# Gate products of a gated linear recurrence: three fp32r matmuls of split operands in place of one fp32 matmul

## The chip, the cores and the metric

The kernel runs on one core of one Trainium2 chip. The metric is device time in microseconds (us), the median of three runs. TensorE (PE) multiplies, VectorE (DVE), ScalarE (ACT) and GpSimd (POOL) do elementwise work, and SyncE (SP) issues most of the loads. PEld is TensorE's loading of stationary operands.

## The reference

One layer of a residual block on 256 tokens of width 2048, in fp32: RMSNorm, one wide input projection, three branches (forgetting attention, a recurrence, attention into 256 memory rows), a gated merge, an output projection, and a feed-forward block of hidden width 5632. The change is in the recurrence branch, of width 1024 in 8 blocks of 128:

```
xr = causal_depthwise_conv(lx, w_lru_conv, b_lru_conv)            # 4 taps
r      = sigmoid(einsum('bsni,nij->bsnj', xb, w_a) + b_a)         # xb: xr in 8 blocks of 128
i_gate = sigmoid(einsum('bsni,nij->bsnj', xb, w_x) + b_x)
log_a = 8 * r * log_sigmoid(lam);  a = exp(log_a)
u = sqrt(-expm1(2 * log_a)) * (i_gate * xr)
h_t = a_t * h_(t-1) + u_t                                         # scan over the 256 tokens
y_lru = h * gelu(lg)
```

## The kernel before

**Weights come in units.** A unit is 512 KB of fp32 weights. SP loads it into one of four slots of `raw`; ACT copies it to the high part (`split` on ACT, fp32r, L666), DVE subtracts to get the low part (`split` on DVE, L1021), and TensorE multiplies three of the four combinations of high and low parts. ACT may copy unit u only when TensorE is done with unit u-4 (`act.wait_ge(pe_units, u - 3)`), so the two elementwise engines work up to about four units ahead of TensorE. A unit of the phases of 256 columns, the recurrence's own projections ("lru") among them, is 16 matmuls, for each of four contraction steps two with 512 moving columns and two with 256; a unit of the phases of 512 columns ("mk", "mq", "v", ...) is 12 matmuls of 512 columns. All of them are recorded at L362, in the helper `mm`, and write `psG`.

**The recurrence runs in four instances m = 0 to 3, of 256 channels each.** Instance m has two groups of four units (x-branch, gate branch); what follows on the elementwise engines and the gate products is interleaved by hand with the next eight units. Every engine executes its list in order. In the lists, "offset o" means: behind the split of unit `start + o`, where `start` is the first unit behind those of instance m. TensorE runs the gate products behind the second of these units (`lru_hooks`, `{1: gates_}`), waits for the taps and for the gate weights, and writes them to `psM` with four fp32 matmuls of 256 columns (each is two records in the trace).

The order on ACT and DVE around them, for instance m with m-1 still running:

- offset 0, ACT: `conv0_`, the first tap of the convolution, into `lru_xr` (L769).
- offset 1, DVE: for m-1 `recurrence` and `gated_y` (offset 9 of m-1), then `taps` of m, six operations (L1108); the last one raises `lru_taps`.
- offset 2: ACT split, then for m-1 `lru_hi` (L801). DVE split, then for m-1 `lru_lo` (L1143).
- offset 3: ACT `copy_low` (L674), split, `gelu_square` (L776). DVE `add_low` (L1032), split, nothing more.
- offset 5 and later: ACT `gate_tanh` reads the gate products, and log_a, exps, root, scan and so on follow.

For the first instance, the second memory-attention instance is what is still running: DVE's `attention_lo` (L1097) stands behind the split of offset 3.

POOL's list for an instance is: load the gate weights into `lru_rg` (two DMAs, L1512, behind the gate products of m-1), then two operations of the GeLU polynomial behind `gelu_square` (L1518 and L1520), then `a_sq` (L1522).

Of the kernel before, what the change touches and what calls it, by code (L numbers as in the profile page):

```python
# [6 lines left out]
ALU = mybir.AluOpType  # L7
ACT = mybir.ActivationFunctionType
F32 = mybir.dt.float32
F32R = mybir.dt.float32r  # L10
AX_X = mybir.AxisListType.X

P = 128
T = 256
# [102 lines left out]
def side_count(kind, m, engine, step):  # L117

    return m * LEN[kind][engine] + (BASE[kind][engine] + (STEP[kind][engine][step] if step else 0))


def at(const, i, coef):

    return const if i is None else i * coef + const


def hybrid_layer_kernel(nc, xT, x_rows, memT, first_data, par, shapes_const, w_units, w_ff, w_rg, out):
    with ExitStack() as ctx:
# [4 lines left out]
        def sb(name, shape, offset, dt=F32):  # L133
            return nc.alloc_sbuf_tensor_at(name, shape, dt, offset=SB0 + int(offset))

        def sem(name):
            return ctx.enter_context(nc.semaphore(name))
# [6 lines left out]
        def wide_before(g):  # L144

            return sum(name in WIDE for name, _, _, _ in GROUPS[:g])
# [6 lines left out]
        M0, G_0, T0 = 144 * KB + 256, 176 * KB + 256, 192 * KB + 256  # L153
# [38 lines left out]
        lru = {}  # L192
        for n in ["lg", "rg", "xr", "ra", "a", "aa", "tn", "ix", "hs", "gg"]:
            shape = [P, 2, 2, P] if n == "rg" else [P, 2, T]
            lru[n] = sb(f"lru_{n}", shape, _o)
            _o += 2 * KB

        dec = {n: sb(f"dec_{n}", [8, T], G_0 + (12 + j) * KB) for j, n in enumerate(["z", "e", "u", "r"])}
        dec_l = sb("dec_l", [8, T], T0 + 2 * KB + 512)
# [48 lines left out]
        psM = ctx.enter_context(nc.psum_tensor("psM", [P, 4, 512], F32))  # L248
# [10 lines left out]
        gain_in, par_in, const_in, ff_in, rg_in = sem("gain_in"), sem("par_in"), sem("const_in"), sem("ff_in"), sem("rg_in")  # L259
# [11 lines left out]
        lam_act, lam_dve = sem("lam_act"), sem("lam_dve")  # L271
        c_out, c_in = sem("c_out"), sem("c_in")
        lru_conv0, lru_taps = sem("lru_conv0"), sem("lru_taps")
        gate_ready = sem("gate_ready")
        gated, acc_added, merged_hi, merged_lo = sem("gated"), sem("acc_added"), sem("merged_hi"), sem("merged_lo")
        x_tok_in = sem("x_tok_in")
# [14 lines left out]
        def columns(w):  # L291

            return slice(w * 512, (w + 1) * 512)
# [5 lines left out]
        def is_zero(m):  # L299

            return isinstance(m, int) and m == 0

        def f32(ap):
            return ap.bitcast(F32)
# [55 lines left out]
        def _(pe):  # L360
            def mm(*a, **kw):
                return nc.tensor.matmul(*a, skip_group_check=True, **kw)  # L362
# [62 lines left out]
            def side_waits(**need):  # L425
                for e, v in need.items():
                    if not is_zero(v):
                        pe.wait_ge(side[e], v)

            def done(ins):  # L430
                ins.then_inc(side["pe"], 1)
# [72 lines left out]

            def lru_hooks(m):
                def gates_():
                    pe.wait_ge(rg_in, at(32, m, 32))
                    pe.wait_ge(lru_taps, at(3, m, 3))

                    side_waits(act=side_count("lru", m - 1, "act", "gate_tanh"))  # L510
                    for j in range(2):
                        for b in range(2):
                            ins = mm(psM[:, j, b * T:(b + 1) * T], lru["rg"][:, j, b], lru["xr"][:, b], start=True, stop=True)
                    done(ins)
                return {1: gates_}

# [113 lines left out]
            for t in range(2):  # L630
                for k in range(2):
                    x_hl = hidden_op(FT - 2 + k)
                    for x_part, w_part in ((0, 0), (0, 1), (1, 0)):
                        ins = mm(psG[:, 2 + t, :], x_hl[:, x_part, t * P:t * P + P], W[:, s, 2 * k:2 * k + 2, w_part],
                                 start=False, stop=k == 1 and x_part == 1)
# [23 lines left out]
        def _(act):  # L659
# [16 lines left out]
            def wait(**need):  # L676
                for e, v in need.items():
                    if not is_zero(v):
                        act.wait_ge(side[e], v)

            def done(ins):
                ins.then_inc(side["act"], 1)
# [79 lines left out]
            L = lru  # L762

            def conv0_(kind, m):
# [5 lines left out]
                                               bias=p1("b_lconv", m * 2 + b), scale=p1("w_lconv", m * 2 + (3 * BT + b)))  # L770
                ins.then_inc(lru_conv0, 1)

            def gelu_square(kind, m):
                wait(**{e: side_count("lru", m, e, None) for e in ("pe", "dve", "act", "pool")})
                act.wait_ge(evac_done, at(G0["lru"] + 2, m, 2))
                done(nc.scalar.activation(L["gg"][:], L["lg"][:], ACT.Square))  # L776
# [30 lines left out]
            def decay_ln(kind, m):  # L807
# [2 lines left out]

            softmax = {7: [exp], 10: [weights_copied], 11: [attention_hi]}
            steps_at = {"normed": {3: [norm_squares]}, "turned": {0: [turned_copied]}, "mem": softmax, "fox": softmax,
                        "lru": {0: [conv0_], 3: [gelu_square], 5: [gate_tanh], 7: [exps, gelu_tanh], 9: [lru_root], 10: [lru_hi]},
                        "decay": {6: [decay_exp], 8: [decay_ln]}}
            hooks = build_hooks(steps_at)

# [197 lines left out]
        def _(dve):  # L1014
            V = nc.vector
# [18 lines left out]
            def wait(**need):  # L1034
                for e, v in need.items():
                    if not is_zero(v):
                        dve.wait_ge(side[e], v)

            def done(ins):
                ins.then_inc(side["dve"], 1)  # L1040
# [58 lines left out]
            L = lru  # L1099

            def taps(kind, m):
                for n in (2, 1, 0):
# [6 lines left out]
                                                     L["xr"][:, b], ALU.mult, ALU.add)  # L1109
                    ins.then_inc(lru_taps, 1)  # L1110

            def log_a(kind, m):
                wait(act=side_count("lru", m, "act", "gate_tanh"))
                for b in range(2):
                    ins = V.tensor_scalar(L["ra"][:, b], L["ra"][:, b], 1.0, ls4[:, bass.ds(m * 2 + b, 1)], ALU.add, ALU.mult)
                done(ins)

                done(V.scalar_tensor_tensor(L["ix"][:], L["ix"][:], 1.0, L["xr"][:], ALU.add, ALU.mult))
# [72 lines left out]
            def decay_bias1(kind, m):  # L1191
# [2 lines left out]

            steps_at = {"normed": {3: [norm]}, "mem": {7: [row_max, weights], 11: [attention_lo]},
                        "fox": {7: [row_max, weights], 11: [attention_lo]},
                        "lru": {1: [taps], 6: [log_a], 8: [decay_sq], 9: [recurrence, gated_y], 10: [lru_lo]},
                        "decay": {5: [decay_z], 7: [decay_one_plus], 8: [decay_inverse], 9: [decay_c], 14: [decay_bias0], 15: [decay_bias1]}}
            hooks = build_hooks(steps_at)

# [220 lines left out]
            for w in range(2):  # L1421
                ins = V.memset(up_pad[w][:, :, 0:2], 0.0)
# [54 lines left out]
            for w in range(4):  # L1477
                per = FT // 2
                for u in range(U0["down"] + per * w + 4, U0["down"] + per * (w + 1) + 4):
                    if u == U0["down"] + per * (w + 1) + 3 and w < 3:  # L1480
                        dve.wait_ge(pe_units, u - 3)
                        b = 2 * (w % 2)
# [10 lines left out]
        @block.gpsimd  # L1493
        def _(pool):
            G = nc.gpsimd

            def wait(**need):
                for e, v in need.items():
                    if not is_zero(v):
                        pool.wait_ge(side[e], v)  # L1500

            def done(ins):
                ins.then_inc(side["pool"], 1)


            def load_gates(m):

                if is_zero(m):
                    pool.wait_ge(pe_units, U0["mq"])
                wait(pe=side_count("lru", m, "pe", None))  # L1510
                for j in range(2):
                    G.dma_start(lru["rg"][:, j], w_rg[j, bass.ds(m * 2, 2)].rearrange("b n c -> n b c")).then_inc(rg_in, 16)  # L1512

            L = lru
            def lru_instance(m):
                load_gates(m)
                wait(act=side_count("lru", m, "act", "gelu_square"))
                done(G.tensor_scalar(L["gg"][:], L["gg"][:], GELU_C, 1.0, ALU.mult, ALU.add))  # L1518
                wait(pool=side_count("lru", m, "pool", "gelu_poly"))
                done(G.tensor_tensor(L["gg"][:], L["gg"][:], L["lg"][:], ALU.mult))  # L1520
                wait(act=side_count("lru", m, "act", "exps"))
                done(G.tensor_tensor(L["aa"][:], L["a"][:], L["a"][:], ALU.mult))  # L1522


            for m in range(4):
                lru_instance(m)

            wait(dve=side_count("decay", 0, "dve", "c"))
            G.dma_start(c_rows, dec["u"][:]).then_inc(c_out, 16)
            pool.wait_ge(c_out, 16)  # L1530
            G.dma_start(c_all[:], c_rows.rearrange("(a h) t -> a h t", a=1).to_broadcast([P, 8, T])).then_inc(c_in, 16)

            pool.wait_ge(x_scaled, 4)
            G.dma_start(x_tok[:], x_rows).then_inc(x_tok_in, 16)

            for w in range(3):
                pool.wait_ge(evac_done, G0["down"] + w + 1)
                G.dma_start(out_rows[:, :, columns(w)], x_tok[:, :, columns(w)]).then_inc(out_stored, 16)
            pool.wait_ge(out_stored, 48)
# [96 lines left out]
```

## Time and profile before

| what | value |
|---|---|
| median of 3 runs | 1627.57 us (1627.21 to 1627.66) |
| the profiled execution | 1627.56 us, span of its instructions 1625.8 us |
| PE busy | 1619.8 us (100%), 8564 matmul records |
| DVE, ACT, POOL busy | 1050.5 us, 869.0 us, 25.3 us |
| chain that ended last | PE 99% |

The span runs from the first instruction to the last. An engine's busy time counts its records; a matmul's record is longer than the distance to the next one, since matmuls overlap. The chain that ended last is followed back from the last instruction to what released it at each step, so its pieces on PE give start-to-start times. Of the chain, 96% is weight products into `psG` at L362, 2% products into `psM` at L362, the gate products among them.

### The profile page before, as it was taken

Reading aid. Unit: us, or ns where it says so; the run is one execution under the profiler, and the core shown is the slowest. Engines: PE = TensorE matmul, PEld = TensorE weight load, DVE = VectorE, ACT = ScalarE, POOL = GpSimd, SP = SyncE. Lnnn points to the kernel's source line nnn. Section 1 sums busy time; section 2 is a strip of 40 time slices with the busy share of each in tenths; the row PEclk is TensorE's granted clock in tenths of the full one; section 3 lists DMA queues with packets and bytes.
Section 4 is the critical chain, followed back from the end, with each engine's and each line's share of the span. In section 5 each row is a group of like instructions: output and inputs, shape, how many; then the busy total and the mean of one; then the engine's idle time right before and its main releaser. Section 6 shows DMA issues by size and latency. Waiting matters only on the chain.

```text
span 1625.8 us, 24820 instructions
## 1 busy us (share of the span) xinstructions
PE 1619.8 (100%) x8564; PEld 1391.6 (86%) x8564; DVE 1050.5 (65%) x1257; ACT 869.0 (53%) x1192; POOL 25.3 (2%) x30
## 2 busy tenths in 40 slices
PE   9999999999999999999999999999999999999999
PEld 8888888888888888888888888888888888888887
DVE  6865678655656575565755777777777777544443
ACT  7665676456554544554544655555555555433332
POOL 0000121000000000000000000000000000000000
PEclk9999999999999999999999999999999999999999
DMA  9554455755556555555565555555655655665663
GB/s 349 183 196 152 158 168 188 259 175 157 160 188 194 190 184 194 182 192 193 181 195 184 176 184 193 197 187 184 203 176 188 206 186 186 201 205 194 206 207 115
DMA packets 85280, 309.58 MB, mean 190 GB/s; under 512 B 9832, under 2 KB 10352, under 8 KB 84976
## 3 DMA queue, kind: packets, MB, share of 16 engines
q1 hardware_dynamic: 83952, 303.14, 56.3%
q0 software_dynamic: 1136, 5.78, 1.0%
q8 instruction: 32, 0.52, 0.1%
q14 instruction: 16, 0.13, 0.0%
q10 hardware_dynamic: 144, 0.01, 0.0%
HBM read 306.78 MB, written 2.11 MB: 190 GB/s over the span
## 4 chain that ended last, share of the span: by engine, by line
PE 99%; DMA 0%; ACT 0%; DVE 0%; issue 0%; ACTq 0%
PE psG L362 96%; PE psM L362 2%; PE psM L447 0%; DMA par_sb<-par 0%; PE psM L601 0%; PE psM L483 0%; ACT fox_square L695 0%; PE psM L481 0%; DVE normed L1059 0%; ACT W L666 0%; DVE x_tok L1490 0%; ACT XM L833 0%; ACT head_rms L707 0%; DVE head_rms L1054 0%; ACT L707 0%
## 5 line engine op out<-in xcount | busy, mean ns | idle before, releaser
L1021 DVE TENSOR_TENSOR W<-raw,W 128x1024 fp32r<-128x1024 f32 x566 | 686.5, 1225 | 380.9 <-ACT W L666 378.3
L362 PE MATMUL psG<-X,W 128*128 128x512 f32 (+1 forms) x4864 | 848.5, 336 | 0.0
L362 PEld LDWEIGHTS psG<-X,W 128*128 128x128 f32 x4864 | 741.2, 188 | 104.1
L666 ACT ACTIVATE W<-raw 128x1024 fp32r<-128x1024 f32 x566 | 589.7, 1054 | 392.3 <-PE psG L362 378.8
L362 PE MATMUL psG<-W,hidden 128*128 128x512 f32 x1056 | 239.5, 389 | 0.0
L362 PEld LDWEIGHTS psG<-W,hidden 128*128 128x128 f32 x1056 | 198.2, 188 | 41.0
L362 PE MATMUL psG<-W,X 128*128 128x512 f32 x768 | 178.6, 392 | 0.0
L362 PEld LDWEIGHTS psG<-W,X 128*128 128x128 f32 x768 | 143.5, 188 | 29.5
L674 ACT ACTIVATE low<-psG 128x512 f32<-128x512 f32 x100 | 59.7, 597 | 149.1 <-PE psG L362 149.1
L362 PE MATMUL psG<-Y,W 128*128 x768 | 133.3, 335 | 0.0
L362 PEld LDWEIGHTS psG<-Y,W 128*128 128x128 f32 x768 | 116.9, 188 | 16.0
L1437 DVE SCALAR_TENSOR_TENSOR up_c<-up_pad,par_sb,up_c 128x256 f32<-128x256 f32 x176 | 77.5, 481 | 42.3 <-ACT up_c L974 36.3
L362 PE MATMUL psG<-W,XM 128*128 128x512 f32 x384 | 88.8, 392 | 0.2 <-ACT XM L833 0.2
L362 PE MATMUL psG<-W,merged 128*128 128x512 f32 x384 | 88.1, 390 | 0.0
L362 PEld LDWEIGHTS psG<-W,XM 128*128 128x128 f32 x384 | 72.2, 189 | 15.6 <-ACT XM L833 0.5
L362 PEld LDWEIGHTS psG<-W,merged 128*128 128x128 f32 x384 | 71.8, 188 | 14.7
L974 ACT ACTIVATE up_c<-up_pad,par_sb 128x256 f32<-128x256 f32 x88 | 48.2, 595 | 60.8 <-DVE up_pad L1429 60.8
L1000 ACT ACTIVATE hidden<-up_c 128x512 f32 (+1 forms) x22 | 13.9, 632 | 65.3 <-DVE up_c L1466 65.3
L1032 DVE TENSOR_TENSOR up_pad<-psG,low 128x512 f32<-128x512 f32 x44 | 30.4, 691 | 25.2 <-ACT low L674 25.2
L1032 DVE TENSOR_TENSOR gates<-psG,low 128x512 f32<-128x512 f32 x24 | 16.6, 691 | 27.8 <-ACT low L674 27.8
L1032 DVE TENSOR_TENSOR yd<-psG,low 128x512 f32<-128x512 f32 x24 | 16.6, 691 | 22.6 <-ACT low L674 22.6
L1429 DVE TENSOR_TENSOR up_pad<-up_pad,rstd 128x512 f32<-128x512 f32 x44 | 30.3, 688 | 0.8
(191 smaller groups left out, 553.1 us busy)
## 6 DMA issues: line engine op xcount, KB each, us to landing
raw<-w_units SPq DMA_DIRECT2D x566, 512.0 KB, 4.0
xs<-xT SPq DMA_DIRECT2D x4, 512.0 KB, 8.0
x_tok<-x_rows POOLq DMA_DIRECT2D x1, 2048.0 KB, 12.2
mem_raw<-first_data SPq DMA_DIRECT2D x3, 512.0 KB, 4.8
mem_raw<-memT SPq DMA_DIRECT2D x3, 512.0 KB, 7.9
out<-x_tok POOLq DMA_DIRECT2D x3, 512.0 KB, 4.2
lru_rg<-w_rg POOLq DMA_DIRECT2D x8, 128.0 KB, 3.9
c_all<-c_rows POOLq DMA_DIRECT2D x1, 1024.0 KB, 6.6
```

Of the source, the lines that this page charges most:

```text
L362: return nc.tensor.matmul(*a, skip_group_check=True, **kw)
L666: nc.scalar.activation(W[:, s, :, 0], raw[:, s], ACT.Copy).then_inc(hi_done, 1)
L674: nc.scalar.activation(low[:, g % 2], psG[:, b:b + 2, T:], ACT.Copy).then_inc(low_copied, 1)
L974: ins = nc.scalar.activation(up_c[w][:, t], up_pad[w][:, t, 2:], ACT.Identity, bias=p1("b_fconv", i * 2 + (w * FT + t)), scale=p1("w_fconv ...
L1000: nc.scalar.activation(hidden[:, bass.ds(i * 2, 2), 0, :], up_c[1][:], ACT.Copy).then_inc(hidden_hi, 1)
L1021: V.tensor_tensor(W[:, s, :, 1], raw[:, s], f32(W[:, s, :, 0]), ALU.subtract).then_inc(lo_done, 1)
L1032: V.tensor_tensor(dst, psG[:, b:b + 2, 0:T], low[:, g % 2], ALU.add).then_inc(evac_done, 1)
L1429: V.tensor_tensor(up_pad[w][:, :, 2:], up_pad[w][:, :, 2:], rstd2.rearrange("p (a t) -> p a t", a=1).to_broadcast([P, 2, T]), ALU.mult).th ...
L1437: ins = V.scalar_tensor_tensor(up_c[w][:, t], up_pad[w][:, t, n:n + T], p1("w_fconv", i * 2 + (n * 2 * FT + w * FT + t)), up_c[w][:, t], A ...
```

## The change

The gate weights and the convolved input of the recurrence are split into high and low parts, in two new buffers `lru_w` and `lru_x` (fp32r), and each fp32 gate product becomes three fp32r matmuls of 256 columns (high·high, high·low, low·high), accumulated in the same half of a bank. ACT makes the high parts at offset 2 (two copies of 256 elements per partition for the weights, one of 512 for the input), DVE the low parts at offset 3 (two subtractions of 256, one of 512). TensorE waits for the low parts in place of the loaded weights and the taps. POOL's load of the next gate weights waits for the low weights of the instance before in place of its gate products, and the first load no longer waits for TensorE's steps of the memory attention.

```diff
+        lru_w = sb("lru_w", [P, 2, 2, 2, P], M0 + 89 * 256, F32R)
+        lru_x = sb("lru_x", [P, 2, 2, T], M0 + 105 * 256 + 64, F32R)
...
             def lru_hooks(m):
                 def gates_():
-                    pe.wait_ge(rg_in, at(32, m, 32))
-                    pe.wait_ge(lru_taps, at(3, m, 3))
+                    pe.wait_ge(lru_w_lo, at(1, m, 1))
+                    pe.wait_ge(lru_x_lo, at(1, m, 1))
...
                     for j in range(2):
                         for b in range(2):
-                            ins = mm(psM[:, j, b * T:(b + 1) * T], lru["rg"][:, j, b], lru["xr"][:, b], start=True, stop=True)
+                            for w_part, x_part in ((0, 0), (0, 1), (1, 0)):
+                                ins = mm(psM[:, j, b * T:(b + 1) * T], lru_w[:, j, b, w_part], lru_x[:, b, x_part],
+                                         start=w_part + x_part == 0, stop=w_part == 1)
                     done(ins)
...
+            def gate_weights_hi(kind, m):
+                act.wait_ge(rg_in, at(32, m, 32))
+                for j in range(2):
+                    ins = nc.scalar.activation(lru_w[:, j, :, 0], L["rg"][:, j], ACT.Copy)
+                ins.then_inc(lru_w_hi, 1)
+
+            def gate_input_hi(kind, m):
+                act.wait_ge(lru_taps, at(3, m, 3))
+                nc.scalar.activation(lru_x[:, :, 0], L["xr"][:], ACT.Copy).then_inc(lru_x_hi, 1)
...
-                        "lru": {0: [conv0_], 3: [gelu_square], 5: [gate_tanh], 7: [exps, gelu_tanh], 9: [lru_root], 10: [lru_hi]},
+                        "lru": {0: [conv0_], 2: [gate_weights_hi, gate_input_hi], 3: [gelu_square], 5: [gate_tanh], 7: [exps, gelu_tanh], 9: [lru_root], 10: [lru_hi]},
...
+            def gate_weights_lo(kind, m):
+                dve.wait_ge(lru_w_hi, at(1, m, 1))
+                for j in range(2):
+                    ins = V.tensor_tensor(lru_w[:, j, :, 1], L["rg"][:, j], f32(lru_w[:, j, :, 0]), ALU.subtract)
+                ins.then_inc(lru_w_lo, 1)
+
+            def gate_input_lo(kind, m):
+                dve.wait_ge(lru_x_hi, at(1, m, 1))
+                V.tensor_tensor(lru_x[:, :, 1], L["xr"][:], f32(lru_x[:, :, 0]), ALU.subtract).then_inc(lru_x_lo, 1)
...
-                        "lru": {1: [taps], 6: [log_a], 8: [decay_sq], 9: [recurrence, gated_y], 10: [lru_lo]},
+                        "lru": {1: [taps], 3: [gate_weights_lo, gate_input_lo], 6: [log_a], 8: [decay_sq], 9: [recurrence, gated_y], 10: [lru_lo]},
...
                 if is_zero(m):
                     pool.wait_ge(pe_units, U0["mq"])
-                wait(pe=side_count("lru", m, "pe", None))
+                else:
+                    pool.wait_ge(lru_w_lo, m)
                 for j in range(2):
                     G.dma_start(lru["rg"][:, j], w_rg[j, bass.ds(m * 2, 2)].rearrange("b n c -> n b c")).then_inc(rg_in, 16)
```

## Rows read from the trace of the kernel before

**Rows 1.** Page, part 1: busy time of TensorE, share of the span, instructions.

```profile
PE 1619.8 (100%) x8564; PEld 1391.6 (86%) x8564; DVE 1050.5 (65%) x1257; ACT 869.0 (53%) x1192; POOL 25.3 (2%) x30
```

**Rows 2.** Chain that ended last, in time order: start us, us, what.

```profile
84.38 21.78 PE psG L362 x96
...
184.98 1.73 PE psM L362 x8
186.71 22.30 PE psG L362 x128
209.01 1.73 PE psM L362 x8
...
234.77 22.19 PE psG L362 x120
```

**Rows 3.** Waits of TensorE over the span: us in total, times, longest.

```profile
PE psM L447 <- DVE normed L1059: 1.0, 1, 1.0
```

**Rows 4.** Instructions on the tile of the gate weights: ns min/median/max, first and last start.

```profile
L362 PE MATMUL psM<-lru_xr,lru_rg x32: 377/379/382, 184.8 to 258.3; 128*128 128x256 f32 x32
L1512 POOL DMA_DIRECT2D lru_rg<-w_rg x8: 720/752/847, 180.1 to 245.7; - x8
...
DMA to landing us min/median/max: 2.8/3.9/5.5
```

**Rows 5.** Timeline of DVE: start us, us, instruction, count, idle before.

```profile
180.51 1.23 DVE L1097 TENSOR_TENSOR Y<-psM,Y 128x1024 fp32r<-128x1024 f32 x1 [1.72 <-ACT Y L760]
...
204.25 2.92 DVE L1108 SCALAR_TENSOR_TENSOR lru_xr<-lx_pad,par_sb,lru_xr 128x256 f32<-128x256 f32 x6
207.09 1.22 DVE L1021 TENSOR_TENSOR W<-raw,W 128x1024 fp32r<-128x1024 f32 x1
208.23 0.69 DVE L1143 TENSOR_TENSOR Y<-lru_hs,Y 128x512 f32 x1
208.83 0.68 DVE L1032 TENSOR_TENSOR lru_lg<-psG,low 128x512 f32<-128x512 f32 x1
209.43 1.22 DVE L1021 TENSOR_TENSOR W<-raw,W 128x1024 fp32r<-128x1024 f32 x1
```

**Rows 6.** Timeline of ACT around the second instance's gate products.

```profile
204.47 0.64 ACT L801 ACTIVATE Y<-lru_hs 128x512 f32 x1 [2.53 <-DVE lru_hs L1138]
205.01 0.58 ACT L674 ACTIVATE low<-psG 128x512 f32<-128x512 f32 x1
205.49 1.05 ACT L666 ACTIVATE W<-raw 128x1024 fp32r<-128x1024 f32 x1
```

**Rows 7.** Timeline of POOL in the recurrence.

```profile
182.55 0.61 POOL L1518 TENSOR_SCALAR lru_gg<-lru_gg 128x512 f32<-128x512 f32 x1 [0.90 <-ACT lru_gg L776]
...
210.28 0.84 POOL L1518 TENSOR_SCALAR lru_gg<-lru_gg 128x512 f32<-128x512 f32 x1 [12.72 <-ACT lru_gg L776]
211.21 1.29 POOL L1520 TENSOR_TENSOR lru_gg<-lru_gg,lru_lg 128x512 f32<-128x512 f32 x1
...
259.28 2.33 POOL L1520 TENSOR_TENSOR lru_gg<-lru_gg,lru_lg 128x512 f32<-128x512 f32 x1
```

**Rows 8.** Timeline of DVE beside the last of these POOL operations.

```profile
259.23 3.46 DVE L1021 TENSOR_TENSOR W<-raw,W 128x1024 fp32r<-128x1024 f32 x2 [0.51 <-ACT W L666]
```

**Rows 9.** Chain that ended last, around TensorE's one later wait.

```profile
327.36 1.23 DVE normed L1059
...
328.73 1.06 PE psM L447 x8
...
351.59 0.87 PE psM L447 x8
```

**Rows 10.** Timeline of TensorE, its first instructions.

```profile
1.07 4.21 PE L362 MATMUL psM<-ones 128*128 128x128 f32 x18 [1.07 <-DVE ones L1208]
```

**Rows 11.** Stretches after TensorE's last matmul: busy of PE, PEld, DVE, ACT, POOL, clock, DMA.

```profile
1622.20:1624.60 2.40, 0.00 (x0) 0.00 (x0) 0.68 (x1) 0.00 (x0) 0.00 (x0) 1.00 0.58 219
1624.70:1625.70 1.00, 0.00 (x0) 0.00 (x0) 0.00 (x0) 0.00 (x0) 0.00 (x0) 0.50 0.00 0
```

More of the change, by code:

```diff
@@ L273, in hybrid_layer_kernel @@
         lru_conv0, lru_taps = sem("lru_conv0"), sem("lru_taps")
+        lru_w_hi, lru_w_lo, lru_x_hi, lru_x_lo = sem("lru_w_hi"), sem("lru_w_lo"), sem("lru_x_hi"), sem("lru_x_lo")
         gate_ready = sem("gate_ready")
```

## The prediction

> **What bounds the kernel now.** I read the page's busy times first: TensorE fills the span [rows 1]. The list of its waits then shows, behind the first microseconds, a single one, of 1.0 us near 328 us [rows 3]. So time comes off or on in two ways alone: the start-to-start time of TensorE's own work, or a new wait of TensorE. Everything on ACT, DVE, POOL and the queues is free as long as TensorE doesn't wait for it. The chain in time order gives the start-to-start times: the eight fp32 records of one instance's gate products take 1.73 us, at 184.98 and at 209.01, with 22.30 us of weight products between [rows 2]. No wait stands at any of the four instances, so what feeds the gate products is early now. How early is the question, and the timelines of DVE and ACT answer it: the last tap of the second instance ends at 204.25 + 2.92 = 207.17 [rows 5], and TensorE comes to the gate products at 209.01 [rows 2]. The slack is 1.84 us.
>
> **TensorE's own part.** The profile gives 379 ns to one fp32 record [rows 4], but the records overlap, and the chain has 1.73 / 8 = 0.216 us for one. The new matmuls have fp32r operands and 256 moving columns. Such ones stand in the units of the recurrence's projection, mixed half and half with 512-column ones: 22.30 us for 128 is 0.174 us each, and the 512-column ones alone take 21.78 / 96 = 0.227 us [rows 2]. So one of 256 columns takes 2 x 0.174 - 0.227 = 0.121 us, and twelve take 1.46 us: 0.27 us less per instance, 1.1 us for four. The mixed units change the bank between matmuls and the new ones stay in one half bank for three; no row has that at 256 columns. From above I bound it by the fp32 record's 0.216 us (twelve: 2.59 us, 4.5 us more than my value for four instances), from below by nothing less than half a 512-column one, 0.113 us (0.4 us less for four). I take 0.121, since operands and columns are those of the row.
>
> **The added operations on ACT.** At offset 2 ACT now makes two copies of 256 elements behind `lru_hi`, which starts at 204.47, the next instruction at 205.01 [rows 6]. A copy of 512 took 0.64 us there, so two of 256 take at most 1.3 us, and end before the last tap at 207.17: that wait hides them. The gate weights are there: their two DMAs start right behind `a_sq`, the last pair by 245.7 for an instance whose gate products start near 257, and land in at most 5.5 us [rows 4]. The copy of the input then waits for the last tap and starts near 207.25; the next instruction starts 0.54 us after such a copy and 0.48 us after a `copy_low` (205.01 less 204.47, 205.49 less 205.01) [rows 6]. So `copy_low` moves from 205.01 to about 207.8 and ends near 208.4, and the split of offset 3 moves from 205.49 to about 208.3 and ends near 209.35. In the queue behind the waiting copy are just these two, and DVE waits for both: its `add_low` starts at 208.83 and its split at 209.43 [rows 5]. Both are met, the second by less than 0.1 us. ACT's part costs nothing, and a tenth more of lateness would cost a tenth.
>
> **The added operations on DVE: here the change costs.** The low parts stand behind the split of offset 3. From the taps on DVE works without a gap: split 207.09, `lru_lo` 208.23, `add_low` 208.83, split 209.43 [rows 5]. That last split already starts later than TensorE's arrival at the gate products, and the three new subtractions come after it. The step from one operation to the next is 1.14 us for 1024 elements and 0.60 for 512 [rows 5], so 0.33 for 256. The first low part can start at 209.43 + 1.14 = 210.57, and alone the three would end at 210.57 + 2 x 0.33 + 0.69 = 211.92.
>
> They aren't alone. At 210.28 POOL starts the two GeLU operations of the same instance, which run until 212.5, in a stretch in which DVE is idle now [rows 7]. Where the two engines meet, they take turns: the second POOL operation takes 1.29 us beside an idle DVE, but 2.33 us at 259.28 [rows 7], when DVE's two splits beside it take 3.46 us in place of about 2.36 [rows 8]. The first one takes 0.61 alone and 0.84 when it comes during a split (210.28, split until 210.65) [rows 5, 7]. The sums show a turn by whole instructions: the second split ends at 262.69, which is 1.08 us behind the POOL operation that came before it and ended at 261.61, a whole split less 0.14. With that: POOL's first operation ends at 211.12 and the first subtraction at 211.12 + 0.42 - 0.14 = 211.40. POOL's second arrives at 211.21 during it and, as at 259.28, ends 1.15 us behind the DVE operation that it waited for, at 212.55. The second subtraction ends at 212.83, and the third, started 0.09 us before that, at 213.43. Without turns it would be 211.92; I take 213.43. The Trainium skill's "SBUF — State Buffer", section "SBUF: two separate sides", says the same as a rule: the pair of ports that DVE and GpSimd share is an exclusive lock for a whole instruction. The trace agrees with it at 259.28; by the rule the low input ends where I put it, and without it the total below would be some 4.5 us less.
>
> TensorE then starts 0.14 us after DVE's record (327.36 + 1.23 to 328.73) and loses 0.19 us of overlap on the first matmuls (1.06 in place of 0.87) [rows 9]. The gate products end at 213.43 + 0.14 + 0.19 + 1.46 = 215.22, against 209.01 + 1.73 = 210.74: 4.48 us later. TensorE stands still for about 4.6 us.
>
> **Which instances, and does it add up?** The chain from the end of one instance's gate products to the next one's taps is the same for each (from 186.71 to 207.17), and ACT's splits in it wait for TensorE, so the whole pattern moves with the stall; nothing is caught up, since TensorE has no other wait in this phase to absorb it. The second and third instances cost 4.48 each, the fourth 4.59, because its way without a stall is 22.19 us and not 22.30 [rows 2]. The first is free: there DVE's `attention_lo` starts at 180.51, the split of offset 3 is long done, and the low parts end by 180.51 + 1.14 + 1.35 = 183.0, or 183.6 with a turn of POOL's 0.61 us between [rows 5, 7], before 184.98 [rows 2]; it saves its 0.27. Sum: 2 x 4.48 + 4.59 - 0.27 = 13.3 us. POOL's earlier load for the first instance, and its changed wait, have nothing behind them that TensorE waits for.
>
> **The clock.** No matmul is recorded from 1622.2 on; the granted clock still reads 1.00 until 1624.6 and 0.50 from 1624.7 [rows 11], so a rest of 2.5 us was enough to bring it from 2.4 to 1.2 GHz there. The rest here would be 4.6 us, and I expect the clock to fall in most of the three. What a return costs is seen at the start only: 18 fp32 records of 128 columns take 4.21 us [rows 10]. A full-clock record of as many columns is 0.87 / 8 = 0.109 us [rows 9], so the 18 should take 1.96, and 2.25 us were lost. For each of the three stalls I bound it by 0 and 2.25 us and take 1.5, nearer to the upper end since the rest exceeds 2.5 us: 4.5 us together. The Trainium skill's "TensorE: Matmul & The Clock Gate", section "Why this matters for your kernels", warns that idle gaps between bursts of matmuls throw the clock back to its half; the trace agrees at its end, where the clock reads 0.50.
>
> **Forecast.** The profiled execution took 1627.56 us, its span 1625.8 and 1.8 around it; the median of the runs is 1627.57, so no correction is needed. 1627.56 + 13.3 + 4.5 = 1645.4 us.
>
> **The rivals.**
> (1) Turns as above, but the clock holds: 1640.9 us. For it: a single rest of 4.6 us between dense matmuls is in no row.
> (2) DVE and POOL don't take turns on these small subtractions, or POOL's operations come later than now: low input at 211.92, 3 us of rest, 2 x 2.97 + 3.08 - 0.27 = 8.75, so 1636.3 us, and up to 1643 with the clock's loss. Against it: rows 7 and 8.
> (3) The stall doesn't come: the low parts are made within the 1.84 us behind the last tap, and the kernel is 1.1 us faster, 1626.5 us, within what a measurement can tell. For that DVE would have to make them before the 3.5 us of `split`, `lru_lo`, `add_low` and `split` that the list puts first; the point that decides is whether the third subtraction ends before 209.0. Against it stand the list and [rows 5].
> (4) The new matmuls take 0.216 us each in one half bank: 4.5 us more, about 1650 us with the forecast's other terms.
>
> **How the numbers follow.** The forecast's case (turns, clock falls at least once; 1642 to 1648.5) gets 0.45, rival 1 0.18, rival 2 0.20, rival 3 0.05, rival 4 0.05, and 0.07 is left for what I don't see. The range from 1636.0 to 1649.0 takes in the forecast's case and rivals 1 and 2 and leaves out rivals 3 and 4 and the rest. A measurement of this kernel can tell about 0.2%, 3.3 us, from no change. Only rival 3 is within that: same 0.05, faster 0.01, slower 0.94.
>
> **What would show each step.** In the changed kernel's profile: a wait of TensorE at `psM` for the low input, three times 4 to 5 us, none at the first instance; DVE's two subtractions of 256 with a gap or a long record between them beside POOL's L1520; the gate products as 12 records in about 1.5 us at full clock; a granted clock below 1.00 in the stretch behind each stall. A stall near 3 us would say that the turns are wrong, none at all that the order on DVE was misread, and four stalls that the first instance isn't free.

## The result, and the profile after

The changed kernel takes 1640.43 us, the kernel before 1627.66 us beside it (medians of seven runs each): ratio 1.0078, 95% interval 1.0066 to 1.009. That is 12.8 us more, inside the range of 1636.0 to 1649.0 and 5 us below the forecast of 1645.4. The first profile of the changed kernel fell in a disturbed execution (mean granted clock 0.85), so the rows below are from a second run of the same file, the first experiment (1639.1 us, profiled execution 1639.14, span 1637.4). Line numbers have moved: L362 is L365, L666 is L671, L1021 is L1036; the new subtractions are L1130 (weights) and L1135 (input).

The list of TensorE's waits in the changed kernel, which answers to [rows 3]:

```profile
PE psM L365 <- DVE lru_x L1135: 6.3, 2, 3.2
PE psM L365 <- DVE lru_w L1130: 3.1, 1, 3.1
...
PE psM L450 <- DVE normed L1074: 1.0, 1, 1.0
```

Three waits of 3.1 to 3.2 us are new, all at the gate products. The chain that ended last shows where they stand (start, us, what); [rows 2] are the same places before:

```profile
184.88 1.42 PE psM L365 x12
186.30 11.17 PE psG L365 x64
...
211.78 1.68 PE psM L365 x12
213.45 11.17 PE psG L365 x64
...
238.93 1.63 PE psM L365 x12
240.55 11.16 PE psG L365 x64
...
265.86 2.90 PE psM L365 x12
268.76 23.26 PE psG L365 x96
```

The first instance has no wait, and its products take 1.42 us in place of 1.73. From the end of one instance's products to the end of the next one's it was 24.03 us (186.71 to 210.74) and is 27.15 (186.30 to 213.45), then 27.10, then 28.21 where it was 23.92. The 96 matmuls behind the last take 23.26 us in place of 21.78. The sum is -0.31 + 3.12 + 3.07 + 4.29 + 1.48 = 11.65 us, all of the 11.6 us by which the span grew. The last two terms hold the clock, as the stretches say (PE, PEld, DVE, ACT, POOL, then the granted clock, DMA):

```profile
211.78:213.45 1.67, 1.67 (x13) 1.67 (x14) 1.26 (x1) 1.32 (x2) 1.52 (x2) 1.00 0.74 275
...
265.86:268.76 2.90, 2.90 (x13) 2.90 (x14) 2.17 (x2) 1.34 (x2) 2.82 (x2) 0.50 0.66 237
268.76:271.60 2.84, 2.84 (x9) 2.16 (x8) 0.00 (x0) 1.57 (x4) 1.11 (x1) 0.50 0.83 276
```

Behind the first two waits the clock stays at 2.4 GHz (1.00); behind the third it is at 1.2 GHz (0.50), and twelve products take 2.90 us there.

Why the low input is late is read in the timeline of DVE around the second instance, which answers to [rows 5]:

```profile
203.85 2.93 DVE L1123 SCALAR_TENSOR_TENSOR lru_xr<-lx_pad,par_sb,lru_xr 128x256 f32<-128x256 f32 x6
206.70 1.22 DVE L1036 TENSOR_TENSOR W<-raw,W 128x1024 fp32r<-128x1024 f32 x1
207.84 0.68 DVE L1168 TENSOR_TENSOR Y<-lru_hs,Y 128x512 f32 x1
208.44 0.68 DVE L1047 TENSOR_TENSOR lru_lg<-psG,low 128x512 f32<-128x512 f32 x1
209.04 1.22 DVE L1036 TENSOR_TENSOR W<-raw,W 128x1024 fp32r<-128x1024 f32 x1
210.17 0.75 DVE L1130 TENSOR_TENSOR lru_w<-lru_rg,lru_w 128x256 fp32r<-128x256 f32 x2
210.84 0.68 DVE L1135 TENSOR_TENSOR lru_x<-lru_xr,lru_x 128x512 fp32r<-128x512 f32 x1
```

Four operations stand between the taps and the low parts, without a gap, and the low input ends at 211.52, 7.67 us after the first tap starts. TensorE's matmuls start at 211.78, 0.26 us later. The three subtractions run without a gap too; it is POOL that waits for them (timeline of POOL; [rows 7] before):

```profile
209.89 2.12 POOL L1544 TENSOR_SCALAR lru_gg<-lru_gg 128x512 f32<-128x512 f32 x1 [12.73 <-ACT lru_gg L791]
212.09 1.30 POOL L1546 TENSOR_TENSOR lru_gg<-lru_gg,lru_lg 128x512 f32<-128x512 f32 x1
...
264.12 4.39 POOL L1544 TENSOR_SCALAR lru_gg<-lru_gg 128x512 f32<-128x512 f32 x1 [12.73 <-ACT lru_gg L791]
```

ACT's part, which answers to [rows 6]: the high input starts right behind the last tap, and the two operations behind it come when DVE needs them.

```profile
206.81 0.64 ACT L786 ACTIVATE lru_x<-lru_xr 128x512 fp32r<-128x512 f32 x1 [1.49 <-DVE lru_xr L1123]
207.35 0.58 ACT L679 ACTIVATE low<-psG 128x512 f32<-128x512 f32 x1
207.83 1.05 ACT L671 ACTIVATE W<-raw 128x1024 fp32r<-128x1024 f32 x1
```

### The profile page after: what moved, and what is told of

It is laid out like the page before. It is cut to its first block, busy times and chain, and to the rows that moved or that the text cites. A ratio compares the mean times of both kernels' runs of the same rounds, so it can differ in the third digit from the quotient of the medians.

```text
span 1787.5 us, 24878 instructions
## 1 busy us (share of the span) xinstructions
PE 1775.3 (99%) x8580; PEld 1452.0 (81%) x8580; DVE 1060.1 (59%) x1269; ACT 880.5 (49%) x1204; POOL 28.8 (2%) x30
## 4 chain that ended last, share of the span: by engine, by line
PE 97%; DVE 1%; issue 1%; ACT 1%; DMA 0%; DVEq 0%; ACTq 0%
PE psG L365 93%; PE psM L365 2%; PE psM L450 0%; DVE W L1036 0%; DVE lru_xr L1123 0%; DMA par_sb<-par 0%; PE psM L606 0%; ACT L812 0%; PE psM L486 0%; ACT lru_aa L812 0%; DVE lru_w L1130 0%; DVE lru_hs L1155 0%; DVE lru_ix L1152 0%; ACT fox_square L700 0%; PE psM L484 0%
## 5 line engine op out<-in xcount | busy, mean ns | idle before, releaser
L1036 DVE TENSOR_TENSOR W<-raw,W 128x1024 fp32r<-128x1024 f32 x566 | 690.2, 1227 | 480.6 <-ACT W L671 478.4
L365 PE MATMUL psG<-X,W 128*128 128x512 f32 (+1 forms) x4864 | 922.9, 355 | 0.0
L365 PEld LDWEIGHTS psG<-X,W 128*128 128x128 f32 x4864 | 780.5, 193 | 139.5
L671 ACT ACTIVATE W<-raw 128x1024 fp32r<-128x1024 f32 x566 | 594.4, 1055 | 503.5 <-PE psG L365 494.1
L365 PE MATMUL psG<-W,hidden 128*128 128x512 f32 x1056 | 265.1, 417 | 0.0
L365 PEld LDWEIGHTS psG<-W,hidden 128*128 128x128 f32 x1056 | 202.4, 192 | 62.3
L365 PE MATMUL psG<-W,X 128*128 128x512 f32 x768 | 196.9, 419 | 0.0
L365 PEld LDWEIGHTS psG<-W,X 128*128 128x128 f32 x768 | 146.9, 192 | 44.0
L365 PE MATMUL psG<-Y,W 128*128 x768 | 145.1, 354 | 0.0
L365 PEld LDWEIGHTS psG<-Y,W 128*128 128x128 f32 x768 | 122.9, 192 | 21.9
L365 PE MATMUL psG<-W,XM 128*128 128x512 f32 x384 | 98.1, 420 | 0.4 <-ACT XM L848 0.4
L365 PE MATMUL psG<-W,merged 128*128 128x512 f32 x384 | 97.3, 417 | 0.0
L365 PEld LDWEIGHTS psG<-W,XM 128*128 128x128 f32 x384 | 74.0, 194 | 23.0 <-ACT XM L848 0.7
L365 PEld LDWEIGHTS psG<-W,merged 128*128 128x128 f32 x384 | 73.4, 192 | 22.2
```

The lines of the kernel that those rows point to most:

```text
L671: nc.scalar.activation(W[:, s, :, 0], raw[:, s], ACT.Copy).then_inc(hi_done, 1)
L1036: V.tensor_tensor(W[:, s, :, 1], raw[:, s], f32(W[:, s, :, 0]), ALU.subtract).then_inc(lo_done, 1)
```

## The experiments

In all of them the medians and ratios are against runs of the kernel before on the same chip (1627.40 to 1627.56 us).

**The changed kernel again, for its profile.**

> The changed kernel once more, for a profile at full clock. Order theory: the three low-part subtractions stand behind four other DVE operations, run without a gap, and end 7.7 us after the first tap starts (211.9 in the times of the kernel before); three waits of TensorE of about 3 us cost 8.75 us with the 0.27 us won at the first instance, and the clock falls to 0.50 behind some of them, which costs the other 4 us of about 12.8: some 1640.4 us. Rival, turns theory: DVE and POOL take turns, the low input ends near 213.4, the three waits are 4.5 us each (13.3 us in all), and the granted clock stays at 1.00: 1640.9 us. Second rival, load theory: no long waits, but all units of the recurrence are longer because ACT and DVE have 12 operations more.

Measured: 1639.1 us, ratio 1.0071 (1.0056 to 1.0087). Three waits of 3.13 to 3.18 us, low input 7.67 us behind the first tap, DVE without a gap: the order theory, and against the turns. The clock fell behind one wait in the profiled execution.

**The added work alone.**

```diff
 def gates_():
-    pe.wait_ge(lru_w_lo, at(1, m, 1))
-    pe.wait_ge(lru_x_lo, at(1, m, 1))
+    pe.wait_ge(rg_in, at(32, m, 32))
+    pe.wait_ge(lru_taps, at(3, m, 3))
...
-            for w_part, x_part in ((0, 0), (0, 1), (1, 0)):
-                ins = mm(psM[:, j, b * T:(b + 1) * T], lru_w[:, j, b, w_part], lru_x[:, b, x_part],
-                         start=w_part + x_part == 0, stop=w_part == 1)
+            ins = mm(psM[:, j, b * T:(b + 1) * T], lru["rg"][:, j, b], lru["xr"][:, b], start=True, stop=True)
```

(In this kernel and the next, POOL's load of the gate weights also waits for the gate products of the instance before, as it did.)

> All twelve added ACT and DVE operations stay where the change puts them, but TensorE multiplies in fp32 as before and waits for the taps and the loaded weights as before. Order theory and turns theory: the work alone costs nothing, 1627.7 us, no wait at the gate products. Load theory: most of the 12.8 us stays, above 1635 us.

Measured: 1627.51 us, ratio 0.9999 (0.9989 to 1.0008), no wait at the gate products. Six more operations per instance on ACT and DVE (24 in all, twelve on each engine) cost nothing where TensorE doesn't wait for them. The load theory falls.

**The wait alone.** The products are fp32 as before, the waits are the changed kernel's.

```diff
             pe.wait_ge(lru_w_lo, at(1, m, 1))
             pe.wait_ge(lru_x_lo, at(1, m, 1))
...
-            for w_part, x_part in ((0, 0), (0, 1), (1, 0)):
...
+            ins = mm(psM[:, j, b * T:(b + 1) * T], lru["rg"][:, j, b], lru["xr"][:, b], start=True, stop=True)
```

> TensorE waits for the low parts as in the change, but multiplies in fp32 as before. Order theory and turns theory: the wait alone is the cost; each instance's products take 0.27 us more than in the change, 1.1 us in all: about 1641.5 us. If the new products were part of the cost, it would be below the changed kernel's 1640.4 us.

Measured: 1643.39 us, ratio 1.0094 (1.0079 to 1.0109). The wait brings all of the cost, and the products win some of it back; the waits are the same 3.1 to 3.2 us. It is 2 us more than was expected. One source shows in the profiled execution, the longest of the four (1645.54 us): the products of all three instances behind a wait take 1.7 to 2.2 times the 1.73 us of the first, with a mean granted clock of 0.50 to 0.64 over them. How often the clock fell in the other three isn't shown. That execution also lost time ahead of the first instance, which has nothing to do with the waits: its products start at 186.71, in the kernel before at 184.98 [rows 2].

```profile
186.71 1.73 PE psM L365 x8
...
213.91 3.01 PE psM L365 x8
...
243.00 3.78 PE psM L365 x8
...
273.11 3.48 PE psM L365 x8
```

**Two operations fewer in front.** One change to the order, on DVE:

```diff
-"lru": {1: [taps], 3: [gate_weights_lo, gate_input_lo], ...
+"lru": {1: [taps], 2: [gate_weights_lo, gate_input_lo], ...
```

> The low parts on DVE move from behind the split of offset 3 to behind the split of offset 2: two operations, an add of 0.60 and a split of 1.14 us, no longer stand before them. Order theory: the low input ends 1.74 us earlier, three waits of about 1.4 us in place of 3.1; 2 x 1.23 + 1.34 - 0.27 = 3.5 us of stall, and with a rest that short the clock holds: 1630.9 us. If the clock falls all the same, up to 1634 us. If the order on DVE weren't the cause, it stays at 1639 us.

Measured: 1631.27 us, ratio 1.0024 (1.0014 to 1.0034), waits of 1.40 to 1.45 us, mean granted clock 1.00. Moving two operations of 1.74 us in sum from before the low parts to behind them takes 1.7 us off each wait, and the clock holds after a rest of 1.4 us.

**The clock's share.** The loop over the instances is written out, so that filling products can stand at the second to fourth instance alone. In both kernels the wait for `gate_tanh` of the instance before moves ahead of the filling:

```diff
-with pe.Fori(1, 4) as i:
-    plain("lru", i, lru_hooks(i - 1))
+for i in range(1, 4):
+    plain("lru", i, lru_hooks(i - 1, fill=12 if i > 1 else 0))
...
+for _ in range(fill):
+    mm(psM[:, 3, 0:P], ones[:], ones[:], start=True, stop=True)
 pe.wait_ge(lru_w_lo, at(1, m, 1))
```

> The changed kernel with TensorE's three instances of the recurrence loop written out, and 12 fp32 products of ones by ones (24 records of 0.109 us, 2.6 us) into an unused bank ahead of the wait at the second to fourth instance, so that TensorE works through most of the 3.1 us of rest. Clock theory: the clock stays at 1.00, the stall itself stays, 1627.4 + 8.75 = 1636.2 us, about 3 us below the changed kernel. Rival: the clock costs nothing and the rest of the 11.7 us is stall; then it stays at 1639 us or above.

> The same written-out loop without the filling products, as the other half of the comparison: as the changed kernel, 1639 to 1640 us, with at least one stretch of granted clock 0.50 behind a stall. If writing out the loop alone changes the time, this shows it.

Measured: 1637.24 us with the filling (ratio 1.0059, 1.0046 to 1.0073; five runs from 1636.05 to 1637.66), 1641.15 us without (1.0084, 1.007 to 1.0098; 1638.92 to 1644.26), which is 1 us above what was expected. The timeline of TensorE with the filling shows 24 records and then a rest of 0.38 us only:

```profile
208.54 2.84 PE L365 MATMUL psM<-ones 128*128 128x128 f32 x24
211.77 1.65 PE L365 MATMUL psM<-lru_x,lru_w 128*128 128x256 f32 x12 [0.38 <-DVE lru_x L1136]
```

The low input comes no earlier, TensorE gains no time by the filling, and the kernel is 3.9 us faster, since the clock stays at 1.00 (mean of each of the five runs). Against the changed kernel's own two medians, 1640.43 and 1639.1, it is 3.2 and 1.9 us, so the size is rough; no run with the filling is as long as the shortest without it. Without it the stretches of the profiled execution (1644.26 us) show the wait, in which PE has nothing, and a lower clock behind each of the three:

```profile
210.50:213.40 2.90, 0.00 (x0) 0.00 (x0) 2.81 (x5) 2.60 (x4) 1.72 (x1) 1.00 0.62 195
213.46:216.50 3.04, 3.04 (x17) 2.85 (x18) 2.52 (x2) 2.47 (x5) 1.63 (x2) 0.71 0.42 158
242.03:245.00 2.97, 2.96 (x13) 2.97 (x14) 2.45 (x2) 1.43 (x2) 1.62 (x2) 0.50 0.42 157
270.60:277.00 6.40, 6.40 (x23) 5.63 (x24) 2.12 (x2) 2.85 (x6) 3.88 (x2) 0.56 0.68 234
```

The chain of the same execution gives the price of a fall:

```profile
186.68 1.41 PE psM L365 x12
...
213.46 1.84 PE psM L365 x12
215.31 12.53 PE psG L365 x64
...
242.03 2.88 PE psM L365 x12
244.92 11.47 PE psG L365 x64
```

At full clock the same products and the 64 matmuls behind them take 1.68 + 11.17 and 1.63 + 11.16 us (the changed kernel's chain above), so the first two falls cost 1.5 and 1.6 us. Its products start 1.8 us later at the first instance too (186.68, in the changed kernel 184.88), so not all of its 1644.26 us is wait and clock.

The filled kernel's stalls are what was expected: the products of one instance end 27.02 us behind those of the one before, three times, where it was 24.03, 24.03 and 23.92, which less the 0.31 us won at the first makes 8.8 us. It takes 1 us more than 1636.2 and has 1.1 us of waits for weight units, at 329 and 332 us, which the changed kernel lacks; why they come there is not settled.

**Low parts right behind the taps.**

```diff
-ACT "lru": {0: [conv0_], 2: [gate_weights_hi, gate_input_hi], 3: [gelu_square], ...
+ACT "lru": {0: [conv0_], 1: [gate_weights_hi], 2: [gate_input_hi], 3: [gelu_square], ...
-DVE "lru": {1: [taps], 3: [gate_weights_lo, gate_input_lo], ...
+DVE "lru": {1: [taps, gate_weights_lo, gate_input_lo], ...
```

> The high weights move to offset 1 on ACT, and the three low-part subtractions to right behind the taps on DVE, ahead of the split of offset 2. Order theory: the low input ends near 208.5, before TensorE arrives at 208.7 to 209.0; no wait, no fall of the clock, and the cheaper products show: 1627.7 - 4 x 0.27 = 1626.6 us. Turns theory: the same, since POOL starts later than the low parts end. Load theory: the added operations are all still there, so it stays above 1631 us.

Measured: 1628.14 us, ratio 1.0004 (0.9995 to 1.0013). The 11 us of loss are gone, but 1.5 us more than expected stay: the third and fourth instance wait 0.75 us each. In the timeline of ACT, `gelu_square` waits for DVE's add, which the three subtractions have pushed back, and a load of ACT's function table (`ACT_TABLE_LOAD`, 1.28 us), the splits and `gate_tanh` (L797) queue behind it, so that `gate_tanh` starts 1.25 us later than before (214.65 for 213.40). The recurrence of this instance follows from `gate_tanh`, and on DVE it stands in front of the next instance's taps:

```profile
210.78 0.64 ACT L791 ACTIVATE lru_gg<-lru_lg 128x512 f32<-128x512 f32 x1 [1.66 <-DVE lru_lg L1047]
211.44 1.28 ACT L671 ACT_TABLE_LOAD   x1
212.73 2.01 ACT L671 ACTIVATE W<-raw 128x1024 fp32r<-128x1024 f32 x2
214.65 0.81 ACT L797 ACTIVATE lru_ra<-psM,half_ba 128x256 f32<-128x256 f32 x2
```

**The same, with `gelu_square` one unit later.** Twice, the second time for the interval.

```diff
-ACT "lru": {..., 3: [gelu_square], 5: [gate_tanh], ...
+ACT "lru": {..., 4: [gelu_square], 5: [gate_tanh], ...
```

> The order of the run with the low parts right behind the taps, and gelu_square moved from offset 3 to offset 4 on ACT, so that ACT's next splits don't wait behind it for DVE's later add. In that run the third and fourth instance waited 0.75 us each, because gate_tanh came 1.25 us later on ACT than in the kernel before. If that is the cause: no wait of TensorE at the gate products, 1627.4 - 1.1 = 1626.3 us. If the late load of a weight unit is the cause instead, the two waits of 0.75 us stay: 1628 us.

> The order of the run with the low parts behind the taps and gelu_square at offset 4, once more, for the interval: 1626.4 us, 1.0 us less than the kernel before, of which four cheaper gate products (4 x 0.3 us) are the whole. If it was noise, 1627.4 us.

Measured: 1626.44 us (ratio 0.9994, 0.9985 to 1.0003) and 1626.41 us (0.9992, 0.9983 to 1.0001). `gate_tanh` starts at 212.51 in the first and TensorE has no wait at the gate products in either profile. The load of ACT's function table now stands ahead of `gelu_square`, where ACT has time, and no longer behind its wait for DVE:

```profile
208.78 1.28 ACT L671 ACT_TABLE_LOAD   x1
...
211.05 0.61 ACT L791 ACTIVATE lru_gg<-lru_lg 128x512 f32<-128x512 f32 x1
211.56 1.05 ACT L671 ACTIVATE W<-raw 128x1024 fp32r<-128x1024 f32 x1
212.51 0.82 ACT L797 ACTIVATE lru_ra<-psM,half_ba 128x256 f32<-128x256 f32 x2
```

The chain of the first of the two has the four products alone:

```profile
184.77 1.42 PE psM L365 x12
...
208.49 1.51 PE psM L365 x12
...
232.30 1.51 PE psM L365 x12
...
255.99 1.46 PE psM L365 x12
```

They take 5.90 us in place of 4 x 1.73 = 6.92: 1.02 us less, and the medians are 0.96 and 1.15 us less. This order has the lowest medians of all; each interval by itself still reaches past 1, by 0.0003 and 0.0001, so the gain is about 0.06 to 0.07% and at the edge of what can be told.

**Does the kind of POOL's operation decide who goes first?**

```diff
-done(G.tensor_scalar(L["gg"][:], L["gg"][:], GELU_C, 1.0, ALU.mult, ALU.add))
+done(G.tensor_tensor(L["gg"][:], L["gg"][:], L["lg"][:], ALU.mult))
...
-done(G.tensor_tensor(L["gg"][:], L["gg"][:], L["lg"][:], ALU.mult))
+done(G.tensor_tensor(L["gg"][:], L["gg"][:], L["lg"][:], ALU.add))
```

> The changed kernel with POOL's first GeLU operation turned from one with a scalar into one with two input tensors (square times gate, then plus gate; the constant 0.0447 of the cubic term is left out, so the output differs). In the kernel before, an operation with two inputs got its turn between two DVE splits; in the changed kernel the one with a scalar got none and waited 2.1 us until all three subtractions were through. If the kind of operation decides: the first POOL operation runs between the subtractions, the low input ends about 1.2 us later, the waits grow from 3.1 to about 4.3 us, and the time to 1642.5 us or more. If it doesn't decide: POOL's operation waits again, the waits stay at 3.1 us and the time at 1639 to 1640 us.

Measured: 1640.15 us, ratio 1.0077 (1.0061 to 1.0092), waits of 3.1 to 3.2 us. The operation with two inputs waits as well (timelines of POOL and of DVE):

```profile
209.74 2.80 POOL L1544 TENSOR_TENSOR lru_gg<-lru_gg,lru_lg 128x512 f32<-128x512 f32 x1 [12.76 <-ACT lru_gg L791]
```

```profile
210.03 0.76 DVE L1130 TENSOR_TENSOR lru_w<-lru_rg,lru_w 128x256 fp32r<-128x256 f32 x2
210.70 0.69 DVE L1135 TENSOR_TENSOR lru_x<-lru_xr,lru_x 128x512 fp32r<-128x512 f32 x1
```

The kind doesn't decide. In the same profile POOL's second operation, of the same kind, does get its turn between two splits that follow each other without a gap: it takes 2.14 us in place of 1.29, and the two splits 3.78 in place of 2.36 (the first of them also waits for POOL's first operation to end).

```profile
212.61 2.14 POOL L1546 TENSOR_TENSOR lru_gg<-lru_gg,lru_lg 128x512 f32<-128x512 f32 x1
```

```profile
212.05 3.78 DVE L1036 TENSOR_TENSOR W<-raw,W 128x1024 fp32r<-128x1024 f32 x2 [0.66 <-ACT W L671]
```

## Why the prediction was right, and where it was not

**The main step held.** The time is lost where the prediction put it: DVE's list puts the split, `lru_lo`, the add and another split between the taps and the low parts, and the low input misses TensorE at the second to fourth instance, not at the first. Shown from four sides: the work without the wait costs nothing (1627.51), the wait without the new products costs it all (1643.39), two operations fewer in front take 1.7 us off each wait (1631.27), and the low parts in front of all four, with `gelu_square` out of the way, leave none (1626.4).

**The step that failed is the turns of DVE and POOL.** The prediction took 213.43 for the end of the low input, with POOL's two operations between the subtractions, over 211.92 without. Counted from the first tap these are 9.18 and 7.67 us; measured is 7.67. DVE went through split and all three subtractions, and POOL's first operation took 2.12 us in place of 0.84. That was 1.51 us too much at each of three instances, 4.5 us, about the whole miss. Its evidence was one meeting in the trace of before, POOL getting in between two splits near 259 us [rows 7, 8]. Such turns exist in the later runs too (2.14 us of POOL's second operation in the last experiment, 2.33 us at the fourth instance of the run with two operations fewer in front), but at the three subtractions POOL got none in any profile of the changed kernel's order. What decides between the two outcomes stays open. The prediction named the sign itself, a stall near 3 us: the waits are 3.1 to 3.2 us. What happened was the second rival, with the clock's loss, for which the text gave 1636.3 to 1643. That the measured time lies in the forecast's range is owed to the range, which took this rival in; the forecast's own case, 1642 to 1648.5, missed it. Rival 1's 1640.9 comes nearest to the median by luck: it has turns at the subtractions and a clock that holds, and the runs of the changed kernel show neither.

**The restart** was sized a little low: 0.26 us from DVE's record to the matmuls where 0.14 was taken, and 0.26 us of lost overlap (1.68 less 1.42) where 0.19 was. Each stall cost 3.07 to 3.12 us at full clock against 2.97 in the sum without turns.

**The clock** fell as forecast, though over a shorter rest and not behind each stall; the sum of its loss came near the forecast's although in the profiles some falls were missing and one cost more than its bound. The stalls alone make about -0.31 + 3.12 + 3.07 + 3.2 = 9.1 us (3.2 for the fourth, like the others plus its 0.11); what the median has above that is 12.8 - 9.1 = 3.7 us, where 4.5 was taken, and the filling products give 3.9 us back. It varies between executions: the profile with 1639.14 us has one fall, that with 1644.26 us has three. A single fall cost 1.5 and 1.6 us behind the first two waits of the latter, as taken, but about 2.6 us behind the third wait of the former (4.29 - 3.2 + 1.48), more than the 2.25 us that the prediction set as an upper bound from the kernel's start.

**The products** were right within a tenth of a us: 1.42 to 1.51 us, forecast 1.46. Staying in one half bank for three matmuls has no price that shows. **ACT's part** was right: the copy of the input waits for the tap, and the two operations behind it come just in time.

## What to carry to other kernels

Cheaper matmuls are worth what they save only if their operands are ready as early as before: count, on the engine that makes the operands, every instruction that the order puts between the last input and the new operation, and set it against the slack (here 1.84 us of slack, and 3.5 us of other work put in front of 1.35 us of new work). The new work itself was free; its place in the queue cost 12.8 us, and a better place turned it into a gain of 1.0 us. A stall of TensorE can cost more than its length, so read the granted clock behind it too, and compare several executions, since the clock's share differs between them.

## What the runs showed of the hardware that was not expected

- A POOL operation that meets a gapless row of DVE operations can wait through several of them: POOL's first operation takes 0.61 us beside an idle DVE, 2.12 us behind a split and three subtractions, and 4.39 us at the fourth instance, where two more splits follow without a gap. In other meetings it gets in after one operation (2.33 us at 259.28 in the kernel before, 2.14 us in the last experiment), and the runs don't show what decides. The Trainium skill's "SBUF — State Buffer", section "SBUF: two separate sides", has the port pair that the two engines share held for the whole instruction by whoever starts first; the runs agree that one side blocks, and in the first kind of meeting show it blocked over several instructions.
- After a rest of 3.1 us the clock falls in some cases and not in others of the same execution (one of three at 1639.14 us, three of three at 1644.26 us), and one fall costs 1.5 to 2.6 us; after 1.4 us it didn't fall.
- An instruction that waits on another engine delays what stands behind it by more than its own need: moving one activation of 0.6 us by one unit, and with it a table load of 1.28 us out from behind its wait, took away two waits of 0.75 us on TensorE.
